# Prompt attention of a hybrid decoder step: work units of one query tile and two heads in place of two tiles and one head

## The chip, the core and the metric

The kernel runs on one core of a Trainium2 chip. The metric is the device time of one execution in microseconds: 1833.09 us is the median of three runs of the kernel before (1832.91 to 1834.04). TensorE (PE in the rows) multiplies; VectorE (DVE), ScalarE (ACT) and GpSimd (POOL) do the elementwise work; SyncE (SP) issues most transfers.

## The reference

One inference step of a one-layer trunk over 1024 prompt tokens and 8 samples: a projection, a gMLP mixer, sparse attention, a merge, and a mixture of experts. The change lies in the prompt's attention alone. With 1024 prompt tokens there are 16 selection blocks and 16 are selected, so the "selected" branch is plain causal attention over all keys; the window branch sees the last 512 keys and the compressed branch 63 compressed keys. Per head, with its own gate for each branch:

```python
p_c = masked_softmax(einsum('bqkgd,bnkd->bqkgn', q, kc) * scale, m_c)   # 63 compressed keys
p_s = masked_softmax(einsum('bqkgd,bkqmd->bqkgm', q, ks) * scale, m_s)  # all keys up to the query
p_w = masked_softmax(einsum('bqkgd,bwkd->bqkgw', q, kw) * scale, m_w)   # last 512 keys
out = gates[..., 0:1] * (p_c @ vc) + gates[..., 1:2] * (p_s @ vs) + gates[..., 2:3] * (p_w @ vw)
```

There are 16 query heads in 2 key groups (8 heads each), head width 64, and 8 query tiles of 128 rows.

## The kernel before

`attend_prompt` works on heads in pairs: head j of group 0 and head j of group 1 lie in the two halves of the partitions (`m.RO`), for j = 0 to 7. Precision is kept with a high part and a low part of each operand, both held as fp32r, so each product is two matmuls.

The unit of work before is (head j, tile pair p): tiles 2p and 2p+1 of one head pair, four units for each j, 32 in all. A unit has four *halves*, numbered H: group g = 0 or 1, and branch a = 0 (all keys) or 1 (window). A half has two *jobs* (H, t), one for each of the unit's two tiles. Each half passes through this chain:

- PE `scores` (L2134 high keys, L2136 low keys, L2126 masks) writes one job's scores to PSUM; four banks hold scores.
- DVE `job_max` (L2362), ACT `job_probs` (L2549, exponential with row sum), DVE `reciprocals` (L2368), POOL `scale` (L2702, times reciprocal and gate).
- PE `turn` (L2165) transposes up to four 128x128 blocks into one of three PSUM banks, ACT `high` (L2562) and DVE `low` (L2395) split them into a high and a low part.
- PE `values` (L2191 and, for the compressed branch, L2210) multiplies by the values and sums four halves of a unit in bank 7.
- ACT `values_out` (L2571) copies the finished bank to `out_kept`, ACT `output_half` (L2581) moves the branch part that lies in the wrong half of the partitions, DVE `output` (L2405) adds the two parts into `m.RO`.

Beside it there are 16 compressed steps C (L2103, L2107 on PE, L2330 to L2384 on DVE, L2538 on ACT, L2711 on POOL), and the queries of the next head are split by POOL (`query_highs` L2721, `query_lows` L2732) and moved by ACT (`move_low_queries` L2530, L2531).

A tile i sees i+1 blocks of keys, so tile 2p+1 has one block more than tile 2p. In `values`, a block that both tiles see is one matmul pair of 256 columns (two tiles side by side); a block that only one of them sees is *alone*: a pair of 128 columns. For the halves 9, 10, 11, 13 and 14 of each head (`ALONE_AHEAD`) the alone matmuls are placed between the transposes of the next half.

The order on each engine is written out by hand in a loop over heads (16 halves each); waits are on semaphores. Before the stage the sample attention ends; after it comes `merge_second`, whose first matmuls (L2848) need `o_high` (L541) and `o_low` (L547) made from `m.RO`.

Of the kernel before, what the change touches and what calls it, by code (L numbers as in the profile page):

```python
# [15 lines left out]
P = 128  # L16
# [53 lines left out]
class Memory:  # L70


    def __init__(self, nc, ctx):
# [36 lines left out]
                   for a, at in enumerate((self.at_R3, self.at_RW + 4 * 4352))]  # L110
# [3 lines left out]
        self.q_low = self.parts("query_lows", self.at_RW + 4 * 3840, 256)  # L114
# [5 lines left out]
        self.pt_parts = [[self.parts(f"turned_{n}{b}", at, 1920) for n, at in zip(("high", "low"), places)]  # L120
                         for b, places in enumerate(((self.at_R1 + 4 * 4096, self.at_R3 + 4 * 6176),
                                                     (self.at_R3 + 4 * 2064, self.at_R3 + 4 * 4128)))]
        self.ptc_parts = [self.parts(f"turned_compressed_{n}", self.at_R1 + 4 * at, SEQ)
                          for n, at in (("high", 6016), ("low", 7040))]
# [1338 lines left out]
def high_queries_at_first(m, si, p):  # L1463

    at, cols = queries_at(p, 0)
    m.nc.scalar.copy(m.q_stacks[0:HD, 0, cols], m.RO[0:HD, at])
    m.nc.scalar.copy(m.q_stacks[HD:P, 1, cols], m.RO[HD:P, at]).then_inc(si.s_qh, 1)


def low_queries_at_first(dve, m, si, p):  # L1470

    at, cols = queries_at(p, 0)
    dve.wait_ge(si.s_qh, p + 1)
    m.nc.vector.tensor_tensor(m.q_stacks[HD:P, 0, cols], m.RO[0:HD, at], m.q_stacks[0:HD, 0, cols], ALU.subtract)
    m.nc.vector.tensor_tensor(m.q_stacks[0:HD, 1, cols], m.RO[HD:P, at], m.q_stacks[HD:P, 1, cols],
                              ALU.subtract).then_inc(si.s_q, 1)
# [484 lines left out]
def attend_prompt(nc, m, fw, si, lw, done, block):  # L1961

    NU = TT // 2 * NKV
    NH2 = 2 * NU
    NHALF = QPK * NH2

    SCALED_BEHIND = (0, 7)
    ALONE_AHEAD = (9, 10, 11, 12, 13, 14)

    def half(H):  # L1970

        h = H % NH2
        return H // NH2, h // 4, h // 2 % 2, h % 2

    def first_block(a, i):
        return 0 if a == 0 else max(0, i - WBLK)
# [6 lines left out]
    def width(H, t):  # L1983
        j, p, g, a = half(H)
        return (2 * p + t + 1 - first_block(a, 2 * p + t)) * P

    def first_column(H, t):

        return P if width(H, t) == 5 * P else 0

    def compressed_ahead(H):
        return H % 16 in (0, 4) and 0 <= H < NHALF

    def compressed_of(H):
        return 2 * (H // 16) + (H % 16) // 4

    def scaled_behind(H):

        return compressed_of(H // 16 * 16 + 4 * SCALED_BEHIND.index(H % 16)) if H % 16 in SCALED_BEHIND else None

    def compressed_turn(H):
        return H % 8 == 1

    jobs, turns, scaled = [], [], []
    for H in range(NHALF):
        jobs += [(H, 0), (H, 1)]
        if compressed_turn(H):
            turns.append(("C", H // 8))
        turns += [(H, c) for c in range(-(-len(blocks(H)) // 4))]
        scaled += [(H, 0), (H, 1)]  # L2010
        if scaled_behind(H) is not None:
            scaled.append(("C", scaled_behind(H)))
# [4 lines left out]
    def turns_of(H):  # L2017
        return [G for G, turn in enumerate(turns[:g_of[H, 0] + 4]) if turn[0] == H or (
            turn == ("C", H // 8) and compressed_turn(H))]

    def turned_by(H):
        return turns_of(H)[-1] + 1
# [60 lines left out]
    def _(pe):  # L2083
# [7 lines left out]
        def compressed_scores(c, s):  # L2091

            if not 0 <= c < 2 * QPK:
                return
# [2138 lines left out]
```

## Time and profile before

| what | us |
|---|---|
| median of three runs | 1833.09 |
| the profiled execution, its own time | 1833.64 |
| its span | 1831.9 |
| busy in the span: PE / PE weight loads | 1804.1 / 1618.9 |
| busy in the span: DVE / ACT / POOL | 1181.5 / 934.2 / 460.3 |
| first score matmul of the stage to the last value matmul | 679 to 1148 |

An instruction's time in a row is from its start to its end. On PE, matmuls overlap: what one costs is read from the distance between starts, not from its own time. The same holds, to a lesser degree, on ACT and DVE. Idle time stands in square brackets, or behind the last bar, with the engine and line that ended it.

### The profile page before, as it was taken

Reading aid. Unit: us, or ns where it says so; the run is one execution under the profiler, and the core shown is the slowest. Engines: PE = TensorE matmul, PEld = TensorE weight load, DVE = VectorE, ACT = ScalarE, POOL = GpSimd, SP = SyncE. Lnnn points to the kernel's source line nnn. Section 1 sums busy time; section 2 is a strip of 40 time slices with the busy share of each in tenths; the row PEclk is TensorE's granted clock in tenths of the full one; section 3 lists DMA queues with packets and bytes.
Section 4 is the critical chain, followed back from the end, with each engine's and each line's share of the span. In section 5 each row is a group of like instructions: output and inputs, shape, how many; then the busy total and the mean of one; then the engine's idle time right before and its main releaser. Section 6 shows DMA issues by size and latency. Waiting matters only on the chain.

```text
span 1831.9 us, 32124 instructions
## 1 busy us (share of the span) xinstructions
PE 1804.1 (98%) x11818; PEld 1618.9 (88%) x11819; DVE 1181.5 (64%) x1673; ACT 934.2 (51%) x1574; POOL 460.3 (25%) x627
## 2 busy tenths in 40 slices
PE   8999999999999999999999999999999999999998
PEld 8999999789999978999989999998768888888884
DVE  5744434566131279999999999645486686645756
ACT  4334343103021178888998888311133675545746
POOL 0000000000000016555555554002112444422431
PEclk9999999999999999999999999999999999999999
DMA  5233334314241550000000000525257797876875
GB/s 185 87 100 115 110 93 159 91 35 140 81 134 50 178 163 1 1 2 1 1 2 2 1 1 13 185 70 175 92 198 280 290 392 291 292 272 221 324 238 196
DMA packets 119762, 241.08 MB, mean 132 GB/s; under 512 B 27986, under 2 KB 84858, under 8 KB 113466
## 3 DMA queue, kind: packets, MB, share of 16 engines
q1 hardware_dynamic: 112666, 214.26, 33.4%
q0 software_dynamic: 6976, 25.17, 5.5%
q8 instruction: 81, 1.33, 0.3%
q14 instruction: 39, 0.32, 0.1%
HBM read 193.52 MB, written 45.88 MB: 131 GB/s over the span
## 4 chain that ended last, share of the span: by engine, by line
PE 57%; DVE 3%; ACT 2%; issue 1%; DMA 0%; POOL 0%; POOLq 0%; ACTq 0%; DVEq 0%
PE ps L3734 20%; PE ps L2191 7%; PE ps L2165 7%; PE ps L3316 4%; PE ps L263 4%; PE ps L2134 3%; PE ps L2136 3%; PE ps L3722 1%; PE ps L2126 1%; PE ps L3783 1%; PE ps L2210 1%; PE ps L2107 1%; PE ps L3728 1%; ACT region_w L2549 1%; PE ps L3793 0%
## 5 line engine op out<-in xcount | busy, mean ns | idle before, releaser
L2362 DVE TENSOR_REDUCE small<-ps 128x1 f32<-128x640 f32 (+7 forms) x256 | 176.3, 698 | 10.5 <-PE ps L2126 7.6
L2395 DVE TENSOR_TENSOR turned_low<-ps,turned_high 128x512 fp32r<-128x512 f32 (+2 forms) x304 | 178.0, 608 | 6.2 <-ACT turned_high L2562 4.5
L2562 ACT CAST turned_high<-ps 128x512 fp32r<-128x512 f32 (+2 forms) x304 | 155.4, 533 | 15.5 <-PE ps L2165 12.0
L2702 POOL TENSOR_SCALAR region_w<-region_w,small,gates 128x640 f32<-128x640 f32 (+7 forms) x172 | 138.4, 814 | 94.2 <-DVE small L2368 94.2
L2191 PE MATMUL ps<-turned_high,value_stacks 128*128 128x256 f32 (+1 forms) x608 | 159.2, 292 | 0.5 <-DVE turned_low L2395 0.5
L2191 PE MATMUL ps<-turned_low,value_stacks 128*128 128x256 f32 (+1 forms) x608 | 147.9, 281 | 0.0
L2134 PE MATMUL ps<-key_stacks,query_stacks 128*128 128x256 f32 (+3 forms) x384 | 141.0, 367 | 3.3 <-ACT region_w L2549 2.8
L3734 PE MATMUL ps<-down_parts,hidden_parts 128*128 128x512 f32 x552 | 131.1, 393 | 0.0
L2549 ACT ACTIVATE region_w<-ps,small 128x640 f32<-128x640 f32 (+7 forms) x172 | 121.2, 707 | 17.2 <-PE ps L2165 8.7
L3734 PE MATMUL ps<-up_parts,rows_parts 128*128 128x512 f32 x552 | 129.0, 389 | 0.1
L3734 PE MATMUL ps<-gate_parts,rows_parts 128*128 128x512 f32 x528 | 125.9, 394 | 0.0
L3734 PEld LDWEIGHTS ps<-up_parts,rows_parts 128*128 128x128 f32 x552 | 103.5, 188 | 21.7 <-issue 0.2
L2136 PE MATMUL ps<-key_lows,query_stacks 128*128 128x256 f32 (+3 forms) x384 | 121.3, 327 | 0.0
L3734 PEld LDWEIGHTS ps<-down_parts,hidden_parts 128*128 128x128 f32 x552 | 102.0, 188 | 20.3 <-issue 0.2
L2191 PEld LDWEIGHTS ps<-turned_high,value_stacks 128*128 128x128 f32 x608 | 116.8, 192 | 0.8 <-issue 0.7
L2191 PEld LDWEIGHTS ps<-turned_low,value_stacks 128*128 128x128 f32 x608 | 116.2, 191 | 0.0
L3734 PEld LDWEIGHTS ps<-gate_parts,rows_parts 128*128 128x128 f32 x528 | 97.7, 188 | 19.8
L2165 PE MATMUL ps<-ident,region_w 128*128 128x128 f32 x708 | 111.5, 279 | 1.0 <-DVE turned_low L2395 0.9
L969 POOL TENSOR_SCALAR small<-small 128x1 f32<-128x1 f32 (+1 forms) x9 | 2.1, 228 | 414.1 <-DVE small L957 414.1
L4088 DVE TENSOR_TENSOR down_parts<-region_w,down_parts 128x2048 fp32r<-128x2048 f32 x32 | 72.0, 2288 | 35.9 <-ACT down_parts L3894 34.8
L4088 DVE TENSOR_TENSOR gate_parts<-region_k,gate_parts 128x2048 fp32r<-128x2048 f32 x32 | 71.9, 2285 | 23.2 <-ACT gate_parts L3894 23.2
L3316 PE MATMUL ps<-w_out_high,y_parts 128*128 128x512 f32 x256 | 84.1, 398 | 0.0
(556 smaller groups left out, 4888.4 us busy)
## 6 DMA issues: line engine op xcount, KB each, us to landing
region_k<-in_w_gate SPq DMA_DIRECT2D x16, 2048.0 KB, 9.6
region_k<-in_w_up SPq DMA_DIRECT2D x16, 2048.0 KB, 10.9
region_w<-in_w_down SPq DMA_DIRECT2D x16, 2048.0 KB, 14.1
region_w<-in_w_in SPq DMA_DIRECT2D x14, 512.0 KB, 4.6
region_k<-in_w_in SPq DMA_DIRECT2D x10, 512.0 KB, 4.4
small<-gate_a SPq DMA_DIRECT2D x8, 516.0 KB, 3.5
region_w<-gate_b SPq DMA_DIRECT2D x8, 516.0 KB, 3.8
region_k<-in_x_prompt SPq DMA_DIRECT2D x8, 512.0 KB, 7.4
```

The source lines that it names most:

```text
L2134: nc.tensor.matmul(out, qs[:, g, tile], k1[:, a, g, k0:k0 + w], start=True, stop=False, skip_group_check=True)
L2136: nc.tensor.matmul(out, qs[:, g, tile], k2[a][:, g, k0:k0 + w], start=False, stop=True, skip_group_check=True)
L2165: last = nc.tensor.transpose(m.ps[:, turn_bank(G), r * P:(r + 1) * P], part, m.ident[:])
L2191: return nc.tensor.matmul(m.ps[:, 7, at:at + n * P], vs[:, a, g, b, :], m.pt_parts[H % 2][x][:, r * P:(r + n) * P], start=(a == 0 and (r, ...
L2362: nc.vector.tensor_reduce(nmax[:, n % 4:n % 4 + 1], sc, AX.X, ALU.max, negate=True).then_inc(s_max, 1)
L2395: nc.vector.tensor_tensor(lo, m.ps[:, turn_bank(G), 0:w], hi, ALU.subtract).then_inc(s_lo, 1)
L2549: nc.scalar.activation(probs(H, t), sc, ACT.Exp, bias=nmax[:, n % 4:n % 4 + 1], accum_out=sums[:, H % 4, t:t + 1]).then_inc(s_exp, 1)
L2562: nc.scalar.copy(hi, m.ps[:, turn_bank(G), 0:w]).then_inc(s_hi, 1)
L2702: nc.gpsimd.tensor_scalar(probs(H, t), probs(H, t), rec[:, H % 4, t:t + 1], m.gates[:, 2 * p + t, col:col + 1], ALU.mult, ALU.mult).then_i ...
L3316: last = nc.tensor.matmul(m.ps[0:n, 2 * (i % 2) + c, :], yparts[:, i % 2, a, k, 0:n], wparts[b][:, k, c * 512:(c + 1) * 512], start=(k == ...
L3734: last = nc.tensor.matmul(out, x[:, a, k, :], w[:, b, k, columns], start=(k == 0 and i == 0), stop=(k == count - 1 and i == 2))
L4088: nc.vector.tensor_tensor(wparts[q][:, 1, part], raw_third(m, q)[:, part], wparts[q][:, 0, part], ALU.subtract).then_inc(s_lo[q], 1)
```

## The change

A unit is now (heads 2k and 2k+1 of a group, tile i): one query tile of two heads, eight units for each pair of heads, 32 in all. The two jobs of a half belong to two heads and have the same width. Every block in `values` is then a pair of 256 columns, and `runs`, `alone_ahead`, `first_value`, `value` and the placing of alone matmuls between transposes go. The loop on each engine runs over pairs of heads (32 halves), tiles in the order 0 to 7, and its order is written anew. The buffers of the turned parts belong to the branch a, not to H % 2. `output` goes from VectorE to GpSimd, with a wait for the scalings issued before it and a wait for its own end. A compressed step takes two tiles of two heads; the clamps for rows that see no compressed key (tile 0) are done in 4 of 16 steps, not 8.

```diff
-def queries_at(p, j):
-    return slice(j * NTOK + p * 256, j * NTOK + (p + 1) * 256), slice(p * 256, (p + 1) * 256)
+TILE_OF = (0, 1, 2, 3, 4, 5, 6, 7)
+def queries_of(x, u):
+    j, i = 2 * (u // TT), TILE_OF[u % TT]
+    return x.rearrange("p (j n) -> p j n", n=NTOK)[:, j:j + 2, i * P:(i + 1) * P]
+def query_slot(u):
+    return slice(u % 4 * 256, (u % 4 + 1) * 256)
...
-    NU = TT // 2 * NKV
-    NH2 = 2 * NU
-    NHALF = QPK * NH2
+    UNITS = QPK // 2 * TT
+    NHP = 4 * TT
+    NHALF = 4 * UNITS
...
     def blocks(H):
-        j, p, g, a = half(H)
-        return [(b, t) for b in range(2 * p + 2) for t in range(2) if first_block(a, 2 * p + t) <= b <= 2 * p + t]
+        return [(b, t) for b in range(first_block(H), tile_of(H) + 1) for t in range(2)]
...
         def values(H):
...
-            for r, n in runs(H):
+            out = m.ps[:, 7, g * 256:(g + 1) * 256]
+            for n in range(width(H) // P):
                 for x in range(2):
-                    if (H, r, x) not in alone_ahead(H):
-                        last = value(H, r, x, n)
+                    last = nc.tensor.matmul(out, vs[:, a, g, first_block(H) + n, :], m.pt_parts[a][x][:, n * 256:(n + 1) * 256],
+                                            start=(a == 0 and n == 0 and x == 0), stop=False, skip_group_check=True)
...
-        def output(n):   # on nc.vector
-            dve.wait_ge(s_ot, n + 1)
-            for g in range(NKV):
-                last = nc.vector.tensor_tensor(m.RO[rows[g], at], out_kept[rows[g], g * 256:g * 256 + 256],
-                                               m.RO[rows[g], at], ALU.add)
-            last.then_inc(s_o, 1)
...
+        def output(n, *ahead):   # on nc.gpsimd
+            ro = queries_of(m.RO, n)
+            pool.wait_ge(s_ot, n + 1)
+            pool.wait_ge(s_scaled, scaled_of.get(ahead, scaled_of[NHALF - 1, 1]))
+            for g in range(NKV):
+                last = nc.gpsimd.tensor_tensor(ro[rows[g]], two_heads(out_kept[rows[g], g * 256:g * 256 + 256]), ro[rows[g]],
+                                               ALU.add)
+            last.then_inc(s_o, 1)
+            pool.wait_ge(s_o, n + 1)
...
-        for j in range(-1, QPK + 1):
-            at, c, n = NH2 * j, 2 * j, 4 * j
+        for j in range(-1, QPK // 2 + 1):
+            at, c, n = NHP * j, TT // 2 * j, TT * j
```

How it moves instructions, at three places. TensorE near the end of the first head, tiles 6 and 7: the scores of a light job of the next head, the transposes of half 15 (L2165) with alone value matmuls of half 14 between them (L2191, 128 columns), then the rest of half 14. `turned_high_67` and `turned_low_68` are the buffers of the turned parts, `key_stacks` the keys.

```order
L2134 MATMUL ps<-key_stacks,query_stacks 128x128
L2136 MATMUL ps<-key_lows_61,query_stacks 128x128
L2126 MATMUL ps<-mask_diag,ident_bf 128x128
L2191 MATMUL ps<-turned_high_67,value_stacks 128x128
L2165 MATMUL ps<-ident,region_w 128x128
L2191 MATMUL ps<-turned_low_68,value_stacks 128x128
L2165 MATMUL ps<-ident,region_w 128x128
L2191 MATMUL ps<-turned_high_67,value_stacks 128x256
L2191 MATMUL ps<-turned_low_68,value_stacks 128x256
L2191 MATMUL ps<-turned_high_67,value_stacks 128x256
```

TensorE of the changed kernel at the end of the first pair of heads, where the light tiles of the next pair are scored and turned while the heavy ones are multiplied (L2135, L2137, L2127 scores, L2161 transposes, L2177 values).

```order
L2127 MATMUL ps<-mask_diag,ident_bf 128x128
L2161 MATMUL ps<-ident,region_w 128x128 x2
L2177 MATMUL ps<-turned_high_67,value_stacks 128x256
L2177 MATMUL ps<-turned_low_68,value_stacks 128x256
L2161 MATMUL ps<-ident,region_w 128x128 x2
L2135 MATMUL ps<-key_stacks,query_stacks 128x256
L2137 MATMUL ps<-key_lows_60,query_stacks 128x256
L2127 MATMUL ps<-mask_diag,ident_bf 128x128
L2177 MATMUL ps<-turned_high_69,value_stacks 128x256
L2177 MATMUL ps<-turned_low_70,value_stacks 128x256
```

Transposes now stand in even numbers without values between them, and each block's values are 256 columns wide; a light half has a single pair of them.

GpSimd before, in the first head, from tile pair 0 into tile pair 1 (`region_w` and `region` hold the probabilities).

```order
L2702 TENSOR_SCALAR region_w<-region_w,small,gates 128x128
L2732 TENSOR_TENSOR query_lows<-region,query_stacks 128x256
L2702 TENSOR_SCALAR region_w<-region_w,small,gates 128x256
L2702 TENSOR_SCALAR region_w<-region_w,small,gates 128x384
L2702 TENSOR_SCALAR region_w<-region_w,small,gates 128x512
L2702 TENSOR_SCALAR region<-region,small,gates 128x384
```

GpSimd after, in the first pair of heads at tile 2 (L2922 `scale`, L2940 and L2950 query parts, L2931 compressed scaling, L2961 `output`).

```order
L2950 TENSOR_TENSOR query_lows<-region,query_stacks 128x256
L2922 TENSOR_SCALAR region<-region,small,gates 128x384
L2961 TENSOR_TENSOR region<-region_w,region 64x2x128 x2
L2922 TENSOR_SCALAR region_w<-region_w,small,gates 128x384
L2931 TENSOR_TENSOR small<-small 128x512
L2922 TENSOR_SCALAR region_w<-region_w,small,gates 128x384 x2
L2940 CAST query_stacks<-region 128x256 x2
```

The two additions of an output (64 partitions, two heads of 128 columns each) now stand between scalings on GpSimd.

VectorE before, around one of the 32 outputs that leave it.

```order
L2395 TENSOR_TENSOR turned_low_70<-ps,turned_high_69 128x512
L2405 TENSOR_TENSOR region<-region_w,region 64x256 x2
L2368 RECIPROCAL small<-small 128x2
L2395 TENSOR_TENSOR turned_low_70<-ps,turned_high_69 128x256
L2362 TENSOR_REDUCE small<-ps 128x1 x2
```

Nothing takes the place of L2405 on VectorE in the changed kernel. Over the stage TensorE has 160 value matmuls fewer (1056 instead of 1216), VectorE 72 instructions fewer, GpSimd 64 more, ScalarE the same number.

## Rows read from the trace of the kernel before

**Rows 1.** The page, busy time of each engine over the whole span.

```profile
PE 1804.1 (98%) x11818; PEld 1618.9 (88%) x11819; DVE 1181.5 (64%) x1673; ACT 934.2 (51%) x1574; POOL 460.3 (25%) x627
```

**Rows 2.** Windows of one and seven heads: us; busy PE, PEld, DVE, ACT, POOL; clock.

```profile
757.30:815.15 57.85, 57.68 (x469) 52.79 (x469) 55.47 (x114) 51.55 (x127) 33.30 (x46) 1.00 0.01 2
...
sum 405.10, PE 403.80 PEld 369.76 DVE 388.53 ACT 361.38 POOL 231.60; mean PE 57.69 PEld 52.82 DVE 55.50 ACT 51.63 POOL 33.09
```

**Rows 3.** Waits from 693 to 1150 us: total, times, longest.

```profile
POOL region_w L2702 <- DVE small L2368: 94.2, 64, 3.2
...
PE ps L2165 <- DVE turned_low L2395: 1.3, 7, 0.2
```

**Rows 4.** Groups by shape, TensorE, 680 to 1150 us.

```profile
L2191 PE MATMUL ps<-turned_high,value_stacks 128*128 128x256 f32 x448 | 122.0, 304 | 0.0
...
L2191 PE MATMUL ps<-turned_low,value_stacks 128*128 128x128 f32 x160 | 45.5, 284 | 0.0
...
L2191 PE MATMUL ps<-turned_high,value_stacks 128*128 128x128 f32 x160 | 41.5, 259 | 0.5 <-DVE turned_low L2395 0.5
```

**Rows 5.** Timeline, TensorE, around alone matmuls that stand behind wide ones.

```profile
761.72 0.28 PE L2191 MATMUL ps<-turned_low,value_stacks 128*128 128x256 f32 x1
761.84 0.23 PE L2191 MATMUL ps<-turned_high,value_stacks 128*128 128x128 f32 x1
761.90 0.28 PE L2191 MATMUL ps<-turned_low,value_stacks 128*128 128x128 f32 x1
762.01 0.33 PE L2210 MATMUL ps<-turned_compressed_high,compressed_value_stacks 128*128 128x256 f32 x1
762.18 0.28 PE L2210 MATMUL ps<-turned_compressed_low,compressed_value_stacks 128*128 128x256 f32 x1
```

**Rows 6.** Timeline, TensorE, light scores, then alone matmuls between transposes.

```profile
741.46 0.30 PE L2134 MATMUL ps<-key_stacks,query_stacks 128*128 128x128 f32 x1
...
741.75 0.31 PE L2191 MATMUL ps<-turned_high,value_stacks 128*128 128x128 f32 x1
741.90 0.30 PE L2165 MATMUL ps<-ident,region_w 128*128 128x128 f32 x1
...
742.10 0.30 PE L2165 MATMUL ps<-ident,region_w 128*128 128x128 f32 x1
```

**Rows 7.** Timeline, TensorE, the largest stall of a head, at 871.6 us.

```profile
871.58 0.23 PE L2126 MATMUL ps<-mask_diag,ident_bf 128*128 128x128 bf16 x1
872.00 0.52 PE L2165 MATMUL ps<-ident,region 128*128 128x128 f32 x3 [0.19 <-DVE turned_low L2395]
```

**Rows 8.** Line L2405: nanoseconds shortest, median, longest.

```profile
L2405 DVE TENSOR_TENSOR region<-region_w,region x64: 404/423/1227, 708.5 to 1152.8; 64x256 f32<-64x256 f32 x64
```

**Rows 9.** Groups by shape, VectorE, 680 to 1150 us.

```profile
L2405 DVE TENSOR_TENSOR region<-region_w,region 64x256 f32<-64x256 f32 x62 | 37.8, 610 | 2.1 <-ACT region L2581 1.1
```

**Rows 10.** Groups by shape, GpSimd, 680 to 1150 us.

```profile
L2732 POOL TENSOR_TENSOR query_lows<-region,query_stacks 128x256 fp32r<-128x256 f32 x28 | 20.8, 743 | 19.0 <-ACT query_stacks L2531 18.4
...
L2702 POOL TENSOR_SCALAR region_w<-region_w,small,gates 128x128 f32<-128x128 f32 x22 | 9.8, 448 | 7.0 <-DVE small L2368 7.0
```

**Rows 11.** Timeline, ScalarE, light jobs and casts.

```profile
741.64 0.47 ACT L2549 ACTIVATE region<-ps,small 128x256 f32<-128x256 f32 x1 [0.24 <-DVE small L2362]
...
742.11 0.58 ACT L2562 CAST turned_high<-ps 128x512 fp32r<-128x512 f32 x1
742.57 0.38 ACT L2549 ACTIVATE region_w<-ps,small 128x128 f32<-128x128 f32 x1
...
742.92 0.87 ACT L2562 CAST turned_high<-ps 128x512 fp32r<-128x512 f32 x2
```

**Rows 12.** Timeline, TensorE: the first scores after the ramp's longest wait.

```profile
685.55 0.36 PE L2134 MATMUL ps<-key_stacks,query_stacks 128*128 128x256 f32 x1 [2.48 <-ACT region_w L2549]
```

**Rows 13.** Timeline, VectorE: the last output of the stage.

```profile
1152.40 0.85 DVE L2405 TENSOR_TENSOR region<-region_w,region 64x256 f32<-64x256 f32 x2 [0.61 <-ACT region L2581]
```

**Rows 14.** Windows, in the ramp: columns as in rows 2.

```profile
688.00:692.00 4.00, 3.63 (x20) 2.61 (x18) 2.47 (x6) 2.16 (x8) 4.00 (x9) 0.69 0.00 0
```

More of the change, by code:

```diff
@@ L2015, in attend_prompt @@
     scaled_of = {job: n + 1 for n, job in enumerate(scaled)}
[L2017 to L2019 removed]
     def turned_by(H):
[L2022 removed]
+        return g_of[H, -(-len(blocks(H)) // 4) - 1] + 1
     bank_of, ahead_of = {}, {}
@@ L2147, in turn @@
             G = g_of[what, c]
-            between = alone_ahead(what - 1) if c == 2 and what != "C" else ()
             if what == "C":
@@ new lines, in _ @@
+            scores(at + 21, 1)
+            turn(at + 19, 2)
+            values(at + 18)
+            scores(at + 22, 0)
+            turn(at + 20, 0)
+            turn(at + 20, 1)
+            scores(at + 22, 1)
+            values(at + 19)
+            turn(at + 20, 2)
+            scores(at + 23, 0)
+            scores(at + 23, 1)
+            turn(at + 21, 0)
+            turn(at + 21, 1)
+            turn(at + 21, 2)
+            values(at + 20)
+            turn(at + 22, 0)
+            scores(at + 24, 0)
@@ new lines, in _ @@
+            scores(at + 26, 0)
+            turn(at + 24, 0)
+            scores(at + 26, 1)
+            values(at + 23)
+            turn(at + 24, 1)
+            scores(at + 27, 0)
+            turn(at + 24, 2)
+            turn(at + 24, 3)
+            scores(at + 27, 1)
+            turn("C", c + 3)
+            turn(at + 25, 0)
+            scores(at + 28, 0)
+            turn(at + 25, 1)
+            turn(at + 25, 2)
+            values(at + 24)
+            scores(at + 28, 1)
+            turn(at + 26, 0)
@@ new lines, in _ @@
+            turn(at + 26, 1)
+            turn(at + 26, 2)
+            scores(at + 29, 0)
+            values(at + 25)
+            turn(at + 26, 3)
+            turn(at + 27, 0)
+            scores(at + 29, 1)
+            turn(at + 27, 1)
+            turn(at + 27, 2)
+            scores(at + 30, 0)
+            values(at + 26)
+            turn(at + 28, 0)
+            scores(at + 30, 1)
+            turn(at + 28, 1)
+            turn(at + 28, 2)
+            turn(at + 28, 3)
+            scores(at + 31, 0)
@@ L2315, in _ @@
+            values(at + 29)
+            turn(at + 31, 0)
+            scores(at + 34, 0)
+            scores(at + 34, 1)
+            scores(at + 35, 0)
+            scores(at + 35, 1)
+            turn(at + 31, 1)
+            turn(at + 31, 2)
+            values(at + 30)
+            scores(at + 36, 0)
+            turn(at + 32, 0)
+            scores(at + 36, 1)
+            turn("C", c + 4)
     @block.vector
@@ L2370, in compressed_gain @@
         def compressed_gain(c):
-            if not 0 <= c < 2 * QPK:
+            if not 0 <= c < UNITS // 2:
                 return
-            q, j = c % 2, c // 2
-            done = 5 * j + 3 * q
+            q, tiles, j = c % 2, [TILE_OF[2 * c % TT + s] for s in range(2)], 2 * (2 * c // TT)
+            done = 2 * c + clamps_ahead(c)
             dve.wait_ge(s_cp, c + 1)
@@ L2586, in _ @@
         last_output = NHALF // 4 - 1
-        for j in range(-1, QPK + 1):
-            at, c, n = NH2 * j, 2 * j, 4 * j
+        for j in range(-1, QPK // 2 + 1):
+            at, c, n = NHP * j, TT // 2 * j, TT * j
+            high(at, 0)
+            job_probs(at + 3, 0)
+            job_probs(at + 3, 1)
+            high("C", c)
+            move_low_queries(n - 1)
+            values_out(n - 1)
+            output_half(n - 1)
+            high(at + 1, 0)
             job_probs(at + 4, 0)
```

844 lines of the change are left out of this document (528 added, 316 removed).

## The prediction

> **What bounds the kernel now.** I read the busy line first: over the whole span TensorE is busy 98% and no other engine over two thirds [rows 1]. That share hides the stage that the change touches, so I read windows next. Prompt attention runs head by head with a period of 57.87 us (seven periods are 405.10 us). In it TensorE is busy 57.7, VectorE 55.5, ScalarE 51.6, GpSimd 33.1, at full granted clock [rows 2]. So TensorE and VectorE are both close to their limit (VectorE 96%), and GpSimd has slack: it waits mostly for VectorE's reciprocals, 94.2 us in 64 waits [rows 3]. TensorE's named waits are next to nothing, 1.3 us [rows 3]. The reader should distrust this, since a matmul's row is 0.28 us long while the next starts 0.12 us later [rows 5], and a wait below 0.16 us shows as no idle time. So the costs below are distances between starts.
>
> **Term 1, the alone matmuls.** Before, 1216 value matmuls: 896 of 256 columns (448 high, as many low) and 320 of 128 columns [rows 4]. After, 1056 of 256 columns, counted from the code (66 blocks for a pair of heads and a group, 8 of these, high and low). Columns streamed are the same in total (896 x 256 + 320 x 128 = 1056 x 256), so only the instruction count pays. A wide one takes 0.12 us from start to start (761.72 to 761.84). An alone pair behind wide ones takes 761.84 to 762.01 = 0.17, and the next matmul is then followed after 0.17 and not 0.12, so the pair costs 0.22, or 0.11 each [rows 5]. Between transposes: from one transpose to the next with an alone matmul between it is 0.20 (741.90 to 742.10) [rows 6], while transposes alone follow each other after 0.12 (three in 0.52, the last of them 0.28 long) [rows 7], so an alone one costs 0.085 there. Halves 9, 10, 11, 13 and 14 of each head are placed so: 16 matmuls a head, 128 in all; 192 stand plain. Removed: 192 x 0.11 + 128 x 0.085 = 32.0 us; added: 160 x 0.12 = 19.2; gain 12.8. Plain alone matmuls with a transpose behind them pay no push. If all cost 0.085 the gain is 27.2 - 19.2 = 8.0, if all cost 0.11 it is 16.0. I take 11.5.
>
> The Trainium skill (TensorE: Matmul & The Clock Gate, Back-to-back issue gap) states a sustained spacing of about 81 ns for 128 columns and N/2.4 + 2.5 ns for an isolated one, 109 ns for 256. An estimate from that page would be 320 x 0.081 - 160 x 0.109 = 8.5 us, the low end; the trace's 0.085 between transposes agrees with it, its 0.11 behind wide ones does not.
>
> **Term 2, stalls.** TensorE's work in one head, by steps between starts: 140 transposes x 0.11 to 0.12 = 15.4; 112 wide values x 0.12 = 13.4; 40 alone = 4.0; 16 compressed values = 1.9; compressed scores about 2.2; 32 score jobs about 19.5 (0.29 for a 128-wide one, 741.46 to 741.75 [rows 6], the wider ones estimated by their columns). Sum about 56.4 of 57.87: 1.5 us a head, 12 in the stage, is stall too short to be named. The largest is 0.42 from a mask to a transpose where 0.04 to 0.06 is usual [rows 7]. They sit where a head turns from heavy to light tiles: light tiles give TensorE little work, but each job has a fixed price on the others.
>
> After, light tiles come less often (every 32 halves) but more in a row. ScalarE steps: a 128-wide job 0.35 (742.57 to 742.92, its accumulator read included), a 256-wide one 0.47 (741.64 to 742.11), a 512 cast 0.46 (742.11 to 742.57) [rows 11]; the fixed rest of a unit (values_out, output halves, query moves, its share of a compressed step) about 2.6 by the same kind of steps. Tile 0: 8 x 0.35 + 4 casts of 256 at 0.25 + 2.6 = 6.4 us. TensorE there: 8 x 0.29 + 8 transposes 0.9 + 8 values 0.95 + 0.5 + 0.8 = 5.4. Tile 1: ScalarE 8 x 0.47 + 4 x 0.46 + 2.6 = 8.2, TensorE 7.2. Tile 2: about 10.2 against 10.7. From tile 3 on TensorE leads by 1 to 4 us. So ScalarE holds TensorE up by about 2 us per pair of heads, 8 in four pairs, with another 1 to 2 for handovers: 9.5 after against 12 before, gain 2.5. The bounds: stalls vanish (gain 12), or double (loss 12).
>
> **Term 3, the output.** VectorE loses 64 additions, on average 0.61 us each [rows 9], 39 us, and 8 small clamps: 5 us a head, from 96% to some 88% busy. This buys time only through term 2, since TensorE's work is the floor. GpSimd gains 64 additions. Its own two-input operation on 256 columns takes 0.743 us [rows 10], so 1.5 us a unit, 12 a pair of heads: GpSimd goes from 66 to 78 of about 113 us. Cover: it waits for reciprocals elsewhere [rows 3]. Behind an output stand the scalings of the next halves, and behind these the transposes. Of GpSimd's light tiles: tile 0 has 8 x 0.45 [rows 10] + 1.5 + queries 1.5 + half a compressed scaling 0.5 = 7.1 us against TensorE's 5.4, tile 1 7.9 against 7.2, tile 2 8.8 against 10.7: in all 23.8 against 23.3, just in time. I price it at 0 beyond the stall above; bounds -1 to +30 (rival B). At the end of the stage the last output is on the path into the merge: 0.85 us for two on VectorE [rows 13], 1.5 on GpSimd, so +0.6.
>
> L2405 takes 404 ns at the least, 423 in the median and 1227 at the most [rows 8] with equal shapes: something blocks it in part of its executions. The Trainium skill (SBUF — State Buffer, SBUF: two separate sides) states that VectorE with two SBUF inputs and a GpSimd operation that reads SBUF exclude each other for a whole instruction. By that rule, with which these rows agree, the move frees VectorE of nearly all such clashes, since its remaining large operations read PSUM; it changes nothing in the sum, only who would suffer in rival B.
>
> **Term 4, the ramp.** At the start the pipeline fills with scores of the first halves while the first scaling and the compressed step are awaited; TensorE waits 2.48 us in one piece [rows 12]. Before, the halves that fill it are of tiles 0 to 3, after of tiles 0 and 1, so less work is done under the same latency: about 5.0 us of scores against 3.5, +1.5. The granted clock in 688 to 692 us is 0.69 in the mean, a stretch at 1.2 in place of 2.4 GHz behind that wait [rows 14]; one more such stretch would cost up to 2. Bounds 0 to +4.
>
> **Sum.** -11.5 - 2.5 + 0.6 + 1.5 = -11.9 us. The profiled execution took 1833.64 us; minus 11.9 is 1821.7; it lies 0.5 above the median 1833.09, so I say 1821. All else in the kernel is unchanged.
>
> **Rivals.**
> - B, slower: GpSimd becomes the pace in the light tiles. The place is `output` between the scalings of tiles 0 to 2; it waits for ScalarE's `output_half`, then for its own end, and nothing behind it can scale meanwhile. If each addition there took up to 1.2 us, as L2405 does at its longest [rows 8], and each of three outputs also stood 1.5 us for ScalarE, a pair of heads would lose 3 x (1.0 + 1.5) + 0.5 = 8 us, 32 in all: -11.5 + (32 - 9.5) + 2.1 = +13, 1846. It decides from a loss above 3 us per pair beyond my stall. For it: 23.8 against 23.3 us leaves no slack there. Against: scores run four halves ahead, and heavy tiles before them leave GpSimd idle. The point of no gain is 5.4 us of stall per pair.
> - C, no change: the new order stalls as the balance above would at its worst, 20 to 24 us and not 9.5, as ScalarE and GpSimd both lag in light tiles. Then -11.5 + 12 + 2.1 = +2 to -2: 1833. For it: the light stretch is twice as long as before. Against: its sum of excess is only 2 us per pair.
> - D, more gain: VectorE at 96% was what made the small stalls, and with 88% they go, term 1 at its high end: -16 - 9 + 1 = -24: 1809. For it: the stall named in rows 7 ends on VectorE's `turned_low`. Against: ScalarE's light tiles.
>
> **Chances.** The forecast 0.68, D 0.10, C 0.12, B 0.10. A change of this kernel can be told from none at about 0.2%, 3.7 us. Faster by more: 0.68 + 0.10 + a quarter of C = 0.81; within: most of C, 0.09; slower: B and the rest, 0.10. The range leaves out most of B and the tail of D: 1811 to 1833. The forecast's own range is 1813 to 1828.
>
> **What would show it.** A period per pair of heads of 111.5 to 113 us instead of 115.7; value matmuls 1056, all of 256 columns, 0.12 apart; VectorE busy about 88% of a period; GpSimd about 69%, with its two outputs near 0.75 us each. Light tiles (the first 23 us of a pair) should show gaps on TensorE ended by ScalarE or GpSimd, in all 2 to 3 us per pair. I am wrong if alone matmuls turn out to have cost well under 0.085 us, if the time from the first scores to the first values grows by more than 4 us, or if TensorE waits for L2922 behind L2961.

## The result

The changed kernel took 1836.55 us (median of 20 runs, 1833.49 to 1838.87), the kernel before 1834.03 us beside it (20 runs, 1832.02 to 1835.91). The ratio is 1.0013, with a 95% interval of 1.0007 to 1.0019: no gain, and by its sign a small loss. The prediction was 1821. The profiled execution took 1838.56 us with a span of 1836.8, against 1833.64 and 1831.9.

The page of the changed kernel, busy time of each engine, answers to [rows 1]:

```profile
PE 1796.2 (98%) x11658; PEld 1606.6 (87%) x11659; DVE 1150.6 (63%) x1601; ACT 929.3 (51%) x1574; POOL 508.2 (28%) x691
```

TensorE has 160 matmuls fewer and 7.9 us less busy time, and the time did not follow. A window of one period answers to [rows 2]; a period is now a pair of heads. First the changed kernel, then the kernel before over two of its heads (us; busy PE, PEld, DVE, ACT, POOL; clock):

```profile
806.82:922.72 115.90, 112.73 (x899) 102.10 (x898) 103.41 (x207) 101.93 (x255) 77.33 (x108) 1.00 0.01 2
```

```profile
819.91:935.60 115.69, 115.31 (x938) 105.66 (x938) 111.04 (x225) 103.20 (x253) 66.54 (x93) 1.00 0.01 1
```

This pair of rows is the core of the case. TensorE's busy time fell by 2.6 us, VectorE's by 7.6, and the period rose by 0.2: TensorE's idle time went from 0.4 to 3.2 us. No engine is near the limit of the period but TensorE. VectorE is busy for 89% of it, where before it was 96%.

The idle time is spread over the period. The same view, cut in two: first from the scores of tile 1 to those of tile 3, with the values of tiles 0 and 1, then the rest up to the next tile 1.

```profile
803.50:827.60 24.10, 22.56 (x169) 18.15 (x169) 21.23 (x51) 22.86 (x68) 20.09 (x33) 1.00 0.00 1
827.60:919.40 91.80, 90.21 (x731) 83.98 (x731) 82.17 (x156) 79.07 (x186) 57.25 (x77) 1.00 0.01 2
```

TensorE idles 1.5 us in the 24 us of the light tiles and 1.6 us in the 92 us behind them.

The groups by shape, answering to [rows 4], show that the work itself is as forecast: 1056 value matmuls, all of 256 columns.

```profile
L2177 PE MATMUL ps<-turned_high,value_stacks 128*128 128x256 f32 x528 | 141.7, 302 | 2.7 <-DVE turned_low L2452 1.5 <-ACT region_w L2706 1.2
L2177 PE MATMUL ps<-turned_low,value_stacks 128*128 128x256 f32 x528 | 130.6, 281 | 0.0
```

The waits of the changed kernel from 700 to 1144 us (total, times, longest), those of TensorE and ScalarE that answer to [rows 3]:

```profile
ACT turned_high L2697 <- PE ps L2161: 42.8, 56, 1.6
...
PE ps L2135 <- ACT region_w L2684: 4.2, 7, 0.7
...
PE ps L2135 <- ACT region L2684: 2.5, 5, 0.7
```

and the same view of the kernel before:

```profile
ACT turned_high L2562 <- PE ps L2165: 12.0, 27, 1.0
...
PE ps L2165 <- DVE turned_low L2395: 1.3, 7, 0.2
```

Two things are to be seen. TensorE's scores (L2135) now wait for ScalarE's exponentials (L2684), which before they did visibly only in the ramp [rows 12]. And ScalarE, which makes TensorE late, itself stands 42.8 us at casts (L2697) whose transposes TensorE has not yet made, against 12.0. Each of the two waits for the other in turn, with neither fully busy. That speaks for an order that puts the wrong instruction in front, and against an overload; the rows alone don't prove it, and the experiments below test it.

Two places stand out in every pair of heads, with 0.66 to 0.69 us of TensorE's idle time each. The first is at tile 1, where ScalarE comes to the exponentials only behind `values_out`, the output halves and a cast (start, length, engine, line; idle time before and releaser in brackets):

```profile
921.33 0.48 ACT L2684 ACTIVATE region<-ps,small 128x256 f32<-128x256 f32 x1
...
922.04 0.36 PE L2135 MATMUL ps<-key_stacks,query_stacks 128*128 128x256 f32 x1 [0.69 <-ACT region L2684]
```

The second is at tile 4, a tile of five blocks:

```profile
844.57 0.82 DVE L2418 TENSOR_REDUCE small<-ps 128x1 f32<-128x640 f32 x1
...
845.16 0.59 ACT L2706 COPY region_w<-ps 128x512 f32<-128x512 f32 x1
...
845.65 0.80 ACT L2684 ACTIVATE region<-ps,small 128x640 f32<-128x640 f32 x1
...
845.77 0.23 PE L2127 MATMUL ps<-mask_diag,ident_bf 128*128 128x128 bf16 x1
...
846.68 0.41 PE L2135 MATMUL ps<-key_stacks,query_stacks 128*128 128x384 f32 x1 [0.68 <-ACT region L2684]
```

Job (50, 0)'s scores end at about 843.5. VectorE reaches their maximum only at 844.57, behind a compressed step; the maximum is ready at 845.39, but ScalarE is in `values_out` until 845.75; the exponential ends at 846.5 and frees the PSUM bank that the next scores, which stand next in TensorE's order, want at about 845.8. Behind these scores TensorE's order has the compressed transposes, whose scaling ended at 845.83, and value matmuls.

At the end of the stage, answering to [rows 13]: the last output on GpSimd, the cast behind it, and the merge.

```profile
1151.68 2.17 POOL L2961 TENSOR_TENSOR region<-region_w,region 64x256 f32<-64x256 f32 x2 [9.65 <-issue]
```

```profile
1153.89 2.58 ACT L541 CAST o_high<-region 128x1376 fp32r<-128x1376 f32 x2 [2.33 <-POOL region L2961]
```

```profile
1156.91 0.42 PE L3130 MATMUL ps<-o_high,branch_b_high 128*128 128x344 f32 x1 [1.84 <-DVE o_low L547]
```

```profile
1158.00:1162.00 4.00, 4.00 (x17) 4.00 (x16) 2.63 (x3) 0.37 (x1) 0.00 (x0) 0.57 0.25 98
```

The stage's last value matmul starts at 1146.2 (before 1147.2). This lead of 1.0 us is not the change's work: the first score matmul already started 1.3 us earlier (677.67 against 678.95), behind a stretch from 640 to 642 us in which the profiled execution of the kernel before had a clock of 0.50 and the changed one 1.00. From first score to last value the stage took 468.6 us, and 468.3 before.

The merge then loses the lead. In the changed kernel the wait for the last output stands at the merge's 49th matmul (1156.91), in the kernel before at its 37th (1154.94, 0.91 us of wait); the 49th started at 1156.93 there. Behind the wait the granted clock is 0.57 for the window from 1158 to 1162 us (a stretch at 1.2 in place of 2.4 GHz); there TensorE starts 17 matmuls where the kernel before starts 28, and the changed kernel comes out 1.6 us behind.

### The profile page after: what moved, and what is told of

It is laid out like the page before. It is cut to its first block, busy times and chain, and to the rows that moved or that the text cites. A ratio compares the mean times of both kernels' runs of the same rounds, so it can differ in the third digit from the quotient of the medians.

```text
span 1836.8 us, 31855 instructions
## 1 busy us (share of the span) xinstructions
PE 1796.2 (98%) x11658; PEld 1606.6 (87%) x11659; DVE 1150.6 (63%) x1601; ACT 929.3 (51%) x1574; POOL 508.2 (28%) x691
## 4 chain that ended last, share of the span: by engine, by line
PE 47%; DMA 4%; ACT 4%; DVE 4%; issue 3%; POOL 1%; ACTq 0%; POOLq 0%; DVEq 0%; SPq 0%
PE ps L4016 15%; PE ps L2161 6%; PE ps L2177 6%; PE ps L3598 4%; PE ps L263 4%; PE ps L2135 3%; PE ps L2137 3%; DMA region_w<-in_w_down 2%; DMA x_and_experts<-region_w,row_out 1%; PE ps L4004 1%; PE ps L2127 1%; PE ps L4065 1%; ACT region_w L2684 1%; ACT turned_high L2697 1%; PE ps L2181 1%
## 5 line engine op out<-in xcount | busy, mean ns | idle before, releaser
L2452 DVE TENSOR_TENSOR turned_low<-ps,turned_high 128x512 fp32r<-128x512 f32 (+1 forms) x304 | 182.2, 613 | 28.0 <-ACT turned_high L2697 24.7
L2697 ACT CAST turned_high<-ps 128x512 fp32r<-128x512 f32 (+1 forms) x304 | 156.1, 535 | 46.6 <-PE ps L2161 45.1
L2922 POOL TENSOR_SCALAR region_w<-region_w,small,gates 128x640 f32<-128x640 f32 (+7 forms) x172 | 134.7, 791 | 78.1 <-DVE small L2424 77.1
L2135 PE MATMUL ps<-key_stacks,query_stacks 128*128 128x256 f32 (+3 forms) x384 | 141.6, 369 | 9.5 <-ACT region_w L2684 5.6
L2177 PE MATMUL ps<-turned_high,value_stacks 128*128 128x256 f32 x528 | 141.7, 302 | 2.7 <-DVE turned_low L2452 1.5
L2177 PE MATMUL ps<-turned_low,value_stacks 128*128 128x256 f32 x528 | 130.6, 281 | 0.0
L2684 ACT ACTIVATE region_w<-ps,small 128x640 f32<-128x640 f32 (+7 forms) x172 | 121.7, 711 | 8.6 <-DVE small L2418 5.3
L2137 PE MATMUL ps<-key_lows,query_stacks 128*128 128x256 f32 (+3 forms) x384 | 121.7, 328 | 0.0
L4016 PEld LDWEIGHTS ps<-down_parts,hidden_parts 128*128 128x128 f32 x552 | 102.0, 188 | 20.7 <-DVE down_parts L4370 0.4
L2177 PEld LDWEIGHTS ps<-turned_high,value_stacks 128*128 128x128 f32 x528 | 100.1, 190 | 5.4 <-DVE turned_low L2452 2.8
L2161 PE MATMUL ps<-ident,region_w 128*128 128x128 f32 x710 | 103.0, 275 | 1.1 <-DVE turned_low L2452 0.7
L2177 PEld LDWEIGHTS ps<-turned_low,value_stacks 128*128 128x128 f32 x528 | 99.9, 189 | 0.0
L2135 PEld LDWEIGHTS ps<-key_stacks,query_stacks 128*128 128x128 f32 x384 | 73.4, 191 | 16.4 <-issue 13.5
```

The lines of the kernel that those rows point to most:

```text
L2135: nc.tensor.matmul(out, qs[:, g, tile], k1[:, a, g, k0:k0 + w], start=True, stop=False, skip_group_check=True)
L2137: nc.tensor.matmul(out, qs[:, g, tile], k2[a][:, g, k0:k0 + w], start=False, stop=True, skip_group_check=True)
L2161: last = nc.tensor.transpose(m.ps[:, turn_bank(G), r * P:(r + 1) * P], part, m.ident[:])
L2177: last = nc.tensor.matmul(out, vs[:, a, g, first_block(H) + n, :], m.pt_parts[a][x][:, n * 256:(n + 1) * 256], start=(a == 0 and n == 0 an ...
L2452: nc.vector.tensor_tensor(lo, m.ps[:, turn_bank(G), 0:w], hi, ALU.subtract).then_inc(s_lo, 1)
L2684: nc.scalar.activation(probs(H, t), sc, ACT.Exp, bias=nmax[:, n % 4:n % 4 + 1], accum_out=sums[:, H % 4, t:t + 1]).then_inc(s_exp, 1)
```

## The experiments

All times are medians beside the kernel before in the same session; ratios are to it.

**a_tail_vector.** Only the last output goes back to VectorE, behind its low parts; GpSimd's `output` stops one unit earlier.

```diff
+        output(UNITS - 1, UNITS)
...
-            if not 0 <= n < UNITS:
+            if not 0 <= n < UNITS - 1:
```

> The changed kernel with one edit: the last unit's output (two adds) is made by VectorE again, behind its own low parts; the other 31 stay on GpSimd. In the changed kernel's profile the two adds take 2.17 us on GpSimd at the tail (VectorE's pair took about 0.85 us each before), the merge waits 1.84 us against 0.91, and the granted clock is 0.5 for 3.4 us right behind that wait. Theory: the tail costs about 1 us of wait, and perhaps 1.5 to 2 us more through the low clock behind it, so this runs 1 to 3 us less than the changed kernel (about 1834 to 1835.5). Rival 1: the low clock comes whatever the wait is, and the gain is only the wait's difference, 0.5 to 1 us. Rival 2: nothing (under 0.3 us), because the merge is then held by low(31) as before.

Measured 1834.86 us, 1.0006 (0.9997 to 1.0015). The wait at the merge is 0.94 again, and the clock there stays at 1.00. It is 1.3 us less than the changed kernel by the ratios, but the two intervals overlap: the sign fits, the size is not settled.

**a_outputs_vector.** All 32 outputs on VectorE, put between its reciprocals and maxima; one of the eight a pair of heads:

```diff
             reciprocals(at + 9)
+            output(n)
...
-            output(n, at + 8, 1)
```

> The changed kernel with all 32 outputs made by VectorE (two adds each, SBUF to SBUF), written in its order where outputs stood between reciprocals and maxima; GpSimd keeps only masks, sums and its share of parts. Rival theory (GpSimd's output, or its contention with VectorE, is what ate the gain): this would give 5 us or more back, below 1832. My theory (the stalls come from the orders, not from the engine that adds): VectorE gets 62 adds of about 0.4 to 0.8 us more, 27 to 38 us over the stage on an engine that is busy 83 to 88 per cent of it, so the time goes up, by 2 to 12 us (1838 to 1848), or stays within 1 us of the changed kernel if VectorE's slack takes them.

Measured 1856.61 us, 1.0117 (1.0102 to 1.0133): 19 us more than the changed kernel (by ratio), beyond the upper end of what I expected. The period is 122.2 us, of which VectorE is busy 108.9:

```profile
812.82:935.02 122.20, 114.42 (x898) 103.90 (x897) 108.91 (x223) 102.53 (x254) 68.41 (x92) 0.99 0.01 2
```

VectorE was given 5.5 us a period and the period grew by 6.3, while VectorE still idles 13. So VectorE's load by itself does not explain the loss; that the additions stood at places where they held up what TensorE wants is the likely reading, and no run here moves them elsewhere. The rival, that GpSimd's outputs ate the gain, asked for a time below 1832 and is not borne out, but this kernel prices its places and not the engine alone; b_pool, below, comes closer to that.

**a_split.** The last blocks' wide value matmuls are made in halves: 320 narrow ones in place of 160 wide, same sums. This undoes term 1 and leaves the new orders.

```diff
+                    alone = n > 0 and n == width(H) // P - 1 and (a == 0 or tile_of(H) in SPLIT)
+                    for t in range(2) if alone else (None,):
+                        cols = slice(0, 256) if t is None else slice(t * P, (t + 1) * P)
```

> The changed kernel with 160 of the alone tiles' wide value matmuls (256 columns) split into 320 narrow ones of 128 columns, same sums; orders untouched. Term 1 as I read it in both traces: a narrow one costs 0.11 us and a wide one 0.12, so 160 more instructions cost 160 x 2 x 0.11 - 160 x 0.12 = 16 us of matmul time, less what hides in stalls: +8 to +16 us, 1844.5 to 1852.5. Rival (the wide matmuls saved nothing, a wide one costs its two narrow halves in TensorE time): within 1 us of the changed kernel, 1835.5 to 1837.5. A result of +10 or more shows that the saving of term 1 is real and is lost in stalls elsewhere.

Measured 1848.23 us, 1.0071 (1.0058 to 1.0085), 10.6 us more than the changed kernel by the ratios, 11.7 by the medians, inside the 8 to 16 expected. Term 1 is real.

**a_order.** Eight pairs of neighbours change places, five on ScalarE and three on VectorE; two of them:

```diff
-            job_probs(at + 8, 1)
             values_out(n)
+            job_probs(at + 8, 1)
...
-            job_max(at + 35, 0)
             low(at + 31, 1)
+            job_max(at + 35, 0)
```

> The changed kernel with eight neighbours exchanged in the written orders of ScalarE (five) and VectorE (three), no work added or taken: ScalarE makes the exponentials at at+8, at+10 and at+26 and the high parts at at+10 and at+15 at places where TensorE was found waiting for them behind another instruction, VectorE likewise the low parts at at+30, at+31 and at+32 ahead of the maxima. Theory (the new orders put the wrong instruction in front, some 22.5 us of stalls between 700 and 1144 us of the profile against 12.4 before): 4 to 12 us faster than the changed kernel, 1824 to 1832.5, with fewer waits of the scores on the exponentials and of the values on the low parts. Rival (ScalarE and VectorE are simply late on average, whatever the order; the wait moves to the next instruction): within 1.5 us of the changed kernel, or slower.

Measured 1834.47 us, 1.0004 (0.9995 to 1.0013): 1.7 us less than the changed kernel by the ratios, near the rival's value and short of my theory's 4 to 12. The waits show why. After the edit (700 to 1144 us):

```profile
PE ps L2135 <- ACT region_w L2684: 5.4, 8, 1.0
...
PE ps L2177 <- DVE turned_low L2452: 0.9, 4, 0.2
```

The value matmuls' wait for low parts fell from 1.5 us (7 waits in the changed kernel) to 0.9, and the scores' wait for exponentials rose from 4.2 to 5.4 (the row on `region` went from 2.5 to 2.3). The two large waits of a pair of heads grew, from 0.68 to 0.95 us at tile 4 and from 0.69 to 1.02 us at tile 1, while smaller ones went: TensorE came sooner to the places that held it before. Single exchanges do not tell an order's fault from an engine's limit, so the next kernel wrote all four orders anew.

**a_orders_new.** The last output on VectorE, and the four loops of the stage with the same calls, each kind in its old sequence, interleaved otherwise (183 lines stand elsewhere). I placed them with a small model of the pipeline whose durations and lags were taken from the changed kernel's trace. At the place shown above, TensorE before and after:

```diff
             scores(at + 18, 0)
-            values(at + 15)
-            turn(at + 16, 2)
+            turn(at + 16, 0)
+            values(at + 14)
+            turn(at + 16, 1)
             scores(at + 18, 1)
+            turn(at + 16, 2)
+            values(at + 15)
+            turn("C", c + 2)
             scores(at + 19, 0)
-            turn("C", c + 2)
```

and ScalarE makes `values_out(n + 3)` behind both exponentials of `at + 18` instead of ahead of them.

> The changed kernel with the last output on VectorE (as in a_tail_vector) and the four written orders of the stage (TensorE, VectorE, ScalarE, GpSimd) written anew: the same instructions per pair of heads, each kind in its old sequence among its own, only interleaved otherwise, so that each instruction stands where the durations and the lags of the changed kernel's trace have its input ready. In windows of one pair the changed kernel's TensorE is busy 112.7 of 115.9 us and idle 3.2. Theory (the idle time is made by which instruction stands in front, not by the load of any engine: VectorE is busy 103.4 of 115.9, ScalarE 101.9, GpSimd 77.3): the idle time falls to about 1 us or less a pair and the kernel to 1821 to 1828 us, faster than the kernel before. Rival 1 (the eight exchanges showed it: a wait taken away comes back at the next instruction, because VectorE and ScalarE together are the bound): within 2 us of a_tail_vector, 1833 to 1836. Rival 2 (orders fitted to one trace are worse than those written by hand): 1838 or more.

Measured 1819.75 us (1819.12 to 1821.35), 0.9923 (0.9910 to 0.9937): 14 us faster than the kernel before, 16.5 faster than the changed kernel by the ratios. One period:

```profile
802.79:914.89 112.10, 111.09 (x899) 101.18 (x897) 102.17 (x206) 101.96 (x254) 77.93 (x109) 1.00 0.01 2
```

Every engine has the work it had (ScalarE 102.0 us, GpSimd 77.9), VectorE is busier in share, and TensorE's idle time fell from 3.2 to 1.0. That is 2.2 of the 3.8 us by which the period fell. The other 1.6 came out of TensorE's busy time, 112.7 to 111.1 with the same matmuls. A wait below about 0.16 us shows as busy time, so these were most likely short waits; the rows can't tell them from work. The idle time went at both kinds of places, to 0.8 us in the light tiles and to 0.3 in the rest:

```profile
799.60:823.70 24.10, 23.33 (x179) 19.34 (x179) 22.32 (x54) 23.58 (x69) 19.71 (x33) 1.00 0.00 1
823.70:911.70 88.00, 87.75 (x722) 81.83 (x721) 79.84 (x154) 78.41 (x185) 58.24 (x77) 1.00 0.01 2
```

ScalarE's wait for transposes fell too (this row from 700 to 1135 us):

```profile
ACT turned_high L2709 <- PE ps L2161: 17.8, 33, 1.3
```

At the same job, the scores no longer wait:

```profile
838.81 0.81 DVE L2418 TENSOR_REDUCE small<-ps 128x1 f32<-128x640 f32 x1
...
839.72 0.79 ACT L2696 ACTIVATE region<-ps,small 128x640 f32<-128x640 f32 x1
...
840.50 0.60 PE L2161 MATMUL ps<-ident,small 128*128 128x128 f32 x4
...
840.85 0.42 PE L2135 MATMUL ps<-key_stacks,query_stacks 128*128 128x384 f32 x1
```

The exponential starts 0.1 us behind the maximum, and TensorE fills the time with value matmuls and the compressed transposes. The theory of the orders holds and "VectorE and ScalarE are the bound" falls. The time lies below the 1821 to 1828 us expected.

**b_plain.** The kernel before, with its alone matmuls straight behind the wide ones.

```diff
-    ALONE_AHEAD = (9, 10, 11, 12, 13, 14)
+    ALONE_AHEAD = ()
```

> The kernel before with the alone tiles' matmuls no longer placed between other work in six of its places but straight behind the wide ones. Term 1 by the rows of before: alone matmuls between scores and transposes cost 0.085 instead of 0.11 us each, 128 x 0.025 = 3.2 us, so 1835.5 to 1838; the stalls are as before. Rival (the interleaving only moved the cost, or it also fills waits whose cover is now gone): no change (1834), or 8 us and more.

Measured 1834.46 us, 1.0003 (0.9993 to 1.0012): no difference, the rival's value and not the 3 us more that the two prices gave. Between transposes an alone matmul starts sooner behind its predecessor, and the transposes start later. Over two periods the mean distance from the start before is 78 ns for alone matmuls in the kernel before and 90 ns here; for transposes it is 116 and 112 ns. The sum over all matmuls of the two periods is 231.4 us in both.

**b_pool.** The kernel before, with outputs 0 to 30 on GpSimd, as the changed kernel has them; one of the four a head:

```diff
-            output(n)
...
+            output(n, at + 9, 1)
```

> The kernel before with outputs 0 to 30 added by GpSimd, behind a scaling, each followed by a wait for its own end, as in the changed kernel; the last one stays on VectorE; all orders else as before. VectorE is busy 111.0 of 115.7 us a pair in the kernel before and would be relieved of some 8 x 2 x 0.45 = 7 us. Term 3 as predicted (nothing in the stage): within 1 us of 1834. Rival 1 (a relieved VectorE shortens the 12 us of stalls by itself): 1826 to 1832. Rival 2 (1.5 us of GpSimd in front of a scaling holds the transposes up, and that is what the changed kernel suffers from): 1838 to 1846.

Measured 1832.24 us, 0.9988 (0.9979 to 0.9997): 2.2 us less. The period goes from 115.7 to 114.9 us, with VectorE down to 101.7:

```profile
808.63:923.54 114.91, 114.48 (x939) 105.32 (x938) 101.68 (x209) 102.67 (x253) 76.53 (x108) 1.00 0.01 1
```

It was expected within 1 us of 1834, and lies between that and the 1826 to 1832 of the first rival. So this part of the change, by itself and in the orders of the kernel before, is a small gain; the rival by which a scaling behind an output holds up the transposes asked for 1838 or more.

**a_orders_tensor and a_orders_others.** The orders of one side alone written anew, each fitted by itself to the orders that stay: TensorE's (31 lines stand elsewhere), and the other three (107). They are not a_orders_new cut in two; the orders differ from those that stand there.

> The changed kernel with the last output on VectorE and only TensorE's written order of the stage made anew (31 lines stand elsewhere); VectorE, ScalarE and GpSimd keep the changed kernel's orders. a_orders_new, with all four anew, took 1819.8 us against 1834.9 of a_tail_vector, TensorE's idle time in a pair of heads going from 3.2 to 1.0 us and its busy time from 112.7 to 111.1. If the fault lies mainly in TensorE's own order (it reaches for its scores and transposes too soon behind their inputs): about half of the 15 us, 1825 to 1830. If the orders of VectorE and ScalarE are at fault: under 3 us, 1832 to 1835.

> The counterpart: TensorE's order as in the changed kernel, the orders of VectorE, ScalarE and GpSimd anew (107 lines stand elsewhere), last output on VectorE. If those three are at fault: 1822 to 1828. If TensorE's own order is the larger part: 2 to 7 us less than a_tail_vector, 1828 to 1833.

Measured 1828.88 us, 0.9972 (0.9961 to 0.9982), and 1829.30 us, 0.9972 (0.9962 to 0.9983). Each side gives about 6 us against a_tail_vector, a_orders_new 15. Both times lie in the ranges that stood for TensorE's order as the larger part, yet the two sides come out equal: neither was the culprit alone. Refitted together they give a little more than the two added (12), by a difference near the noise of these runs.

**a_orders_split.** a_orders_new with a_split's edit.

> a_orders_new (1819.8 us) with 160 of the wide value matmuls of the last blocks split into 320 narrow ones, as a_split did to the changed kernel (there +11.7 us by the medians). Theory (term 1 is real and by itself worth about 11.5 us, and good orders alone do not beat the kernel before by much): +9 to +13 us, 1829 to 1833. Rival (with good orders the narrow ones hide, so that the gain of a_orders_new is all a matter of orders): within 3 us of 1819.8.

Measured 1830.05 us, 0.9978 (0.9969 to 0.9987), 10.3 us more than a_orders_new by the medians and 10.1 by the ratios. With good orders the wide matmuls are worth the same as with bad ones.

**a_orders_new2.** The orders fitted once more, to a_orders_new's own trace.

> a_orders_new with the four orders worked over once more by the durations and lags of its own trace, where 1.0 us a pair is left idle on TensorE. If what is left can be taken too: 1 to 3 us less, 1817 to 1819. If the rest is a matter of lags that no order hides: 1819 to 1821.

Measured 1821.98 us, 0.9937 (0.9923 to 0.9950), and its period is 112.56 us against 112.10. Fitting further did not pay: the first expectation fell, and the time lies 1 us above the range of the second. a_orders_new is the version that beats both kernels.

## Why the prediction was wrong

The step that failed is **term 2, stalls**. The prediction let them go from 12 to 9.5 us, by adding up what ScalarE and TensorE each have to do in a light tile, and it gave the tiles from 3 on next to nothing (1 to 2 us in the stage for handovers), since TensorE leads there by 1 to 4 us. TensorE's idle time is 3.2 - 0.4 = 2.8 us a pair of heads more, 11 us in four pairs: -2.5 became about +11. Of the 3.1 us that the two windows of a period show, 1.5 lie in the light tiles, near the 2 us that the sum had there and ended in the main by ScalarE as it said; 1.6 lie behind them, 0.68 in one piece at a tile of five blocks. A balance of loads says nothing of these: a_orders_new has the same loads in each tile and idles 1.0, with 1.6 us less busy time besides. Rival C gave 20 to 24 us of stall, with a chance of 0.12. Its size (12 + 11 = 23) and its number (1833 to within 4 us) came true; its reason, the light tiles, holds for half of the visible idle time. A loss in the orders themselves was no rival of the prediction.

- **Term 1, the alone matmuls**, -11.5 predicted: right. Busy time fell by 2.6 us a pair, 10.3 in four, and since short waits can hide in busy time the proof is in the runs: a_split costs 10.6, a_orders_split 10.3. The two prices that it mixed were not both true: b_plain finds no gain in the placing, so the 0.085 us of [rows 6] was the alone matmul's share only, and its neighbours paid the rest. With 0.12 for a wide one, (10.3 + 160 x 0.12) / 320 gives 0.092 us for any of them. The estimate from the Trainium skill (TensorE: Matmul & The Clock Gate, Back-to-back issue gap), 8.5 us, was nearer in this than the other end, 16.
- **Term 3, the output**: in the stage priced at 0, and measured at -2.2 us in the kernel before (b_pool). Rival B did not happen: no matmul of the changed kernel waits visibly for a scaling (L2922), and weight loads do so 7 times, 2.0 us in all, from 700 to 1144 us. (Its own sum took 9.5 from its 32 us where the 12 of the kernel before belong: +10.6 and 1844, not +13 and 1846.) At the tail priced at +0.6. The pair of additions took 2.17 us, not 1.5, and the merge waited 1.84 instead of 0.91; with the clock behind it the lead of 1.0 us became a lag of 1.6, by differences along TensorE's instructions: 2.6 us where 0.6 was priced. Given back to VectorE, the outputs cost 19 us at the places where I put them; that says as much of the places as of the engine.
- **Term 4, the ramp**, +1.5 predicted. From the first score matmul to the last value matmul it is 468.3 us before and 468.6 after; four periods are 462.8 and 463.6 of them, so ramp and drain together take 5.5 and 5.0. They shrank by about 0.5, and the first value matmul came 11.1 us behind the first score and not 14.3, though the granted clock was 0.50 from 684 to 688 and 0.66 from 688 to 692 us, a longer stretch than [rows 14] belongs to.
- **The signs named**: matmul count and shape, VectorE near 88% (89%), GpSimd near 69% (67%) and its additions near 0.75 us (0.73 in the median) came as said; light tiles showed 1.5 us of gaps and not 2 to 3; the period of 111.5 to 113 did not, and that was the sign that the forecast hung on. a_orders_new has it: 112.1.

Sum by what was measured: -10.3 + 11.2 for the stage's periods, -0.5 for ramp and drain, +2.6 at the tail, about +3; the medians differ by 2.5. The profiled execution lies 4.9 above that of before: -1.3 ahead of the stage, +0.3 in it, +2.6 at the tail, and some 3 net between 1335 and 1367 us, in a stage that the change does not touch, where the clock was 0.60 and 0.55 in two windows; the kernel before had such a stretch at 1335. The first and the last of the four lie outside the stage and belong to these single executions.

What is not settled: whether the low clock behind the tail's wait comes in every execution. The changed kernel has one profile, with it, and a_tail_vector one, without. And no run refits the orders of the kernel before, which had 12 us of stall by the prediction's count. So the 14 us by which a_orders_new beats it are not all the new units': with narrow matmuls put back and the outputs left on GpSimd (a_orders_split) 4 of them stay.

## What to carry to other kernels

When work is taken from the engine that sets the pace, its partners have to be ready earlier by as much, and a written order has to be fitted again to the new durations. Sum the saving and ask in a separate sum who is ready when, instruction by instruction; a balance of busy time per tile can't answer it. Here the mark of an order at fault was two engines that wait for each other at under 90% load, with the same waits at the same places in every period. Exchanging single neighbours moved the wait on; rewriting all the orders together, with a model fed from the trace, took it away, and one side alone (6 of 15 us for either) told less than the whole. Busy time is no floor either: with the same matmuls it fell by 1.6 us a period.

## What had not been expected of the hardware

- The last output's two additions on GpSimd took 1.37 and 0.74 us, 2.17 from first to last, where 0.73 is the median. The first ran beside VectorE's `o_low` (L547, both inputs in SBUF), which ended at 1152.47, 0.59 us ahead of it:

```profile
1148.59 3.87 DVE L547 TENSOR_TENSOR o_low<-region,o_high 128x688 fp32r<-128x688 f32 x3
```

  The Trainium skill (SBUF — State Buffer, SBUF: two separate sides) has the two engines exclude each other for a whole instruction in this case, and the row agrees with it: the addition took its usual time from there on, less 0.14.
- VectorE's additions of the same form took 610 ns on average in the kernel before [rows 9] and 437 in a_outputs_vector:

```profile
L2461 DVE TENSOR_TENSOR region<-region_w,region 64x256 f32<-64x256 f32 x62 | 27.1, 437 | 4.9 <-ACT region L2735 4.0
```

  In the kernel before, 30 of the 62 additions took 0.56 to 1.23 us; each of the 30 began during a GpSimd operation and ended 0.26 to 0.28 us behind the end of that one. The other 32 took 0.40 to 0.43 us, though 16 of them began during one too, and what sets these apart is not settled here. In a_outputs_vector 7 of 64 were long (0.48 to 0.69 us). A duration from one order is no price in another.
